# One more VectorE add, and two fewer TensorE sums, at the five stage changes of a two-layer encoder

## What is computed

```python
def _rmsnorm(x, g):
    xf = x.astype(jnp.float32)
    y = xf * lax.rsqrt(jnp.mean(xf * xf, axis=-1, keepdims=True) + EPS)
    return (y * g.astype(jnp.float32)).astype(x.dtype)
...
u = _modulate(_rmsnorm(x, norm_g[l, 0]), ada[:, 0], ada[:, 1])
x = x + 0.5 * ada[:, 2][:, None, :] * _swiglu(u, w_ff1_up[l], w_ff1_down[l])
```

## Time and profile before

| what | value |
| --- | --- |
| median of 3 runs | 2010.5 us (2010.05 to 2010.67) |
| the profiled execution's own time | 2011.53 us |
| its span in the profile | 2009.7 us |
| TensorE busy | 1997.3 us (99%) |
| VectorE busy | 986.4 us (49%) |
| ScalarE busy | 570.9 us (28%) |
| GpSimd busy | 679.6 us (34%) |
| granted TensorE clock | full level (2.4 GHz) until all of its work is done |

### The profile page before, as it was taken

The page is one execution under the profiler, slowest core; times in us unless marked ns, Lnnn a source line. Parts: engine busy times, 40 slices in busy tenths (PEclk is TensorE's granted clock), DMA queues, the critical chain, the costliest instruction groups (busy, mean ns, idle before and its releaser), DMA issues.

```text
span 2009.7 us, 24346 instructions
## 1 busy us (share of the span) xinstructions
PE 1997.3 (99%) x10051; PEld 1674.6 (83%) x10051; DVE 986.4 (49%) x1407; ACT 570.9 (28%) x837; POOL 679.6 (34%) x278
## 2 busy tenths in 40 slices
PE   8999999999999999999999999999999999999999
PEld 7888888987788888888898888889777898888888
DVE  4964265574465775312266624747643757211121
ACT  3221223234423322122242212224253233211221
POOL 1644346201000445444434644451200006443441
PEclk9999999999999999999999999999999999999999
DMA  9765366422234466333426645663222335323331
GB/s 298 206 213 171 89 198 207 101 74 84 63 99 132 126 187 210 84 105 100 131 84 196 204 134 147 174 202 77 78 74 69 121 105 157 121 82 100 86 119 60
DMA packets 351966, 264.75 MB, mean 132 GB/s; under 512 B 49966, under 2 KB 333794, under 8 KB 351856
## 3 DMA queue, kind: packets, MB, share of 16 engines
q1 hardware_dynamic: 350176, 262.70, 44.0%
q10 hardware_dynamic: 1392, 0.39, 0.1%
q0 software_dynamic: 288, 0.11, 0.0%
HBM read 261.07 MB, written 2.10 MB: 131 GB/s over the span
## 4 chain that ended last, share of the span: by engine, by line
PE 96%; DMA 1%; SPq 1%; DVE 1%; ACT 0%; issue 0%; DVEq 0%; ACTq 0%
PE bank L1535 28%; PE bank L1537 28%; PE bank L1536 28%; PE bank L1620 1%; PE bank L1624 1%; PE bank L1621 1%; PE bank L1562 1%; PE bank L1564 1%; PE bank L1563 1%; PE ps L1740 1%; DMA ada_block<-in_w_ada 1%; PE ps L1719 0%; PE ps L1728 0%; PE ps L1709 0%; SPq L559 0%
## 5 line engine op out<-in xcount | busy, mean ns | idle before, releaser
L660 POOL TENSOR_TENSOR w_lo<-stage,w_hi 128x1024 fp32r<-128x1024 f32 (+1 forms) x236 | 652.2, 2782 | 1158.6 <-ACT w_hi L720 1119.7
L1535 PE MATMUL bank<-u_hi,w_hi 128*128 128x512 f32 x1768 | 694.8, 393 | 1.4 <-DVE u_lo L1329 1.0
L1537 PE MATMUL bank<-u_hi,w_lo 128*128 128x512 f32 x1768 | 688.3, 389 | 0.0
L1536 PE MATMUL bank<-u_lo,w_hi 128*128 128x512 f32 x1768 | 688.0, 389 | 0.0
L720 ACT ACTIVATE w_hi<-stage 128x1024 fp32r<-128x1024 f32 (+2 forms) x335 | 348.4, 1073 | 548.0 <-DMA stage<-in_w_ff_up 292.9
L1535 PEld LDWEIGHTS bank<-u_hi,w_hi 128*128 128x128 f32 x1768 | 331.9, 188 | 73.9 <-issue 3.5
L1537 PEld LDWEIGHTS bank<-u_hi,w_lo 128*128 128x128 f32 x1768 | 331.8, 188 | 69.9
L1536 PEld LDWEIGHTS bank<-u_lo,w_hi 128*128 128x128 f32 x1768 | 332.0, 188 | 69.5 <-issue 1.9
L1535 PE MATMUL bank<-h_hi,w_hi 128*128 128x512 f32 x744 | 289.4, 389 | 0.0
L1536 PE MATMUL bank<-h_lo,w_hi 128*128 128x512 f32 x744 | 289.4, 389 | 0.0
L1537 PE MATMUL bank<-h_hi,w_lo 128*128 128x512 f32 x744 | 289.4, 389 | 0.0
(11 more groups left out here) (218 smaller groups left out, 1429.0 us busy)
## 6 DMA issues: line engine op xcount, KB each, us to landing
stage<-in_w_ff_up SPq DMA_DIRECT2D x172, 512.0 KB
ada_stage<-in_w_ada SPq DMA_DIRECT2D x128, 512.0 KB, 5.2
stage<-in_w_ff_down SPq DMA_DIRECT2D x32, 1408.0 KB
stage<-in_w_in SPq DMA_DIRECT2D x16, 1024.0 KB
ada_block<-in_w_ada SPq DMA_DIRECT2D x8, 1024.0 KB, 11.8
stage<-in_w_out SPq DMA_DIRECT2D x8, 1024.0 KB
stage<-in_w_in SPq DMA_DIRECT2D x40, 128.0 KB
stage<-in_w_in SPq DMA_DIRECT2D x10, 512.0 KB
```

Source lines behind the costliest of these rows:

```text
L660: nc.gpsimd.tensor_tensor(stage_tile(w_lo, kind, n), t, hi_tile(n, depth(kind, n)), ALU.subtract).then_inc(lo_ready, 1)
L1535: mm(bank[n % BANKS][:, :], hi[:, k, :], rhs_hi(k), start=(k == order[0]), stop=False)
L1536: mm(bank[n % BANKS][:, :], hi[:, k, :], rhs_lo(k), start=False, stop=False)
L1537: last = mm(bank[n % BANKS][:, :], lo[:, k, :], rhs_hi(k), start=False, stop=(k == order[-1]))
```

## The change

Three things are changed. VectorE gets a new add: at the head of `to_next` it adds the square of block 7's first half to `sq_sum`. `norm_sum` for the first half then reads `sq_sum` alone and leaves line 1595's two sums out; for the second half it stays as it was. And the place of that sum in pass 2 is step k_n - 3 where it was step 5: that is k = 8 after a feed-forward stage and still k = 5 after mixing. The rest renumbers the semaphore `squares_added`, which now counts eight adds per stage.

```diff
-SUM_K, SPREAD_K, SUM_B_K, SPREAD_B_K = 5, 4, 2, 5
+SPREAD_K, SUM_B_K, SPREAD_B_K = 4, 2, 5
...
             def to_next(l, i, done):
+                add_squares(event(l, i) + 1, KT - 1)
                 stats(*divmod(event(l, i) + 1, 3), 0)
                 close_second(l, i, 0, done)
-                add_squares(event(l, i) + 1, KT - 1)
+                add_squares(event(l, i) + 1, KT)
                 normalise(*divmod(event(l, i) + 1, 3), lambda: close_second(l, i, 1, done))
...
-                frames = slice(0, S) if step < KT - 2 else slice(0, FH) if step == KT - 2 else slice(FH, S)
-                done = {KT - 2: KT - 3, KT - 1: KT - 3}.get(step, step - 1)
-                dve.wait_ge(squared, HX * (e - 1) + (KT + 1 if step == KT - 1 else step + 1))
+                frames = slice(0, S) if step < KT - 2 else slice(FH, S) if step == KT else slice(0, FH)
+                done = {KT - 2: KT - 3, KT - 1: KT - 2, KT: KT - 3}.get(step, step - 1)
+                dve.wait_ge(squared, HX * (e - 1) + step + 1)
                 if done > 0:
-                    dve.wait_ge(squares_added, (KT - 1) * (e - 1) + done)
+                    dve.wait_ge(squares_added, KT * (e - 1) + done)
...
-                        if e < 3 * DEPTH and p == 2 and k == SUM_K:
+                        if e < 3 * DEPTH and p == 2 and k == k_n - 3:
                             norm_sum(e, 0)
...
-                pe.wait_ge(squares_added, (KT - 1) * (e - 1) + KT - 2 + h)
+                pe.wait_ge(squares_added, KT * (e - 1) + KT - 1 + h)
                 for j in (2 * h, 2 * h + 1):
-                    mm(ps5[:, j:j + 1], sq_sum[:, j * P:(j + 1) * P], ones[:, :], start=(j == 2 * h), stop=False,
-                       skip_group_check=True)
+                    last = mm(ps5[:, j:j + 1], sq_sum[:, j * P:(j + 1) * P], ones[:, :], start=(j == 2 * h), stop=(h == 0),
+                              skip_group_check=True)
+                if h == 0:
+                    last.then_inc(norm_summed, 1)
+                    return
                 pe.wait_ge(squared, HX * (e - 1) + KT + 2 * h)
```

More of the change, by code:

```diff
@@ L727, in square @@
                 act.wait_ge(x_updated, x_before(*divmod(e, 3)) - HX + step + 1)
-                added = {KT - 1: KT - 2, KT: KT - 3, KT + 1: KT - 1}.get(step, step - 1)
+                added = {KT - 1: KT - 2, KT: KT - 3, KT + 1: KT}.get(step, step - 1)
                 if added > 0:
-                    act.wait_ge(squares_added, (KT - 1) * (e - 1) + added)
+                    act.wait_ge(squares_added, KT * (e - 1) + added)
                 nc.scalar.activation((squares if m else sq_sum)[:, frames], x_t[:, m, frames], ACT.Square
```

## The result

The changed kernel takes **2015.23 us** (median of 17 runs, 2013.16 to 2017.87) against 2010.55 for the kernel before (17 runs, 2010.02 to 2014.47): 1.0022 times as long, with a 95% interval of 1.0016 to 1.0028. That is 4.7 us more. It lies inside the range (2012.0 to 2015.6) but 1.4 above the forecast of 2013.8. The 0.2% (4.0 us) that I had called "the same" lies within the interval, so on which side of it the change falls is not told. The time is where rival 2, the clock, had put it (2015.1).

What follows compares the result with a forecast made beforehand. TensorE, busy 1997.3 of 2009.7 us, was taken to bound the kernel; the five stage changes summed 1.35 + 0.62 - 0.64 + 1.23 + 0.72 = +3.3 us on 2010.5, giving 2013.8 us, range 2012.0 to 2015.6.

Steps and rivals of the forecast that it cites:

- rival 2: TensorE's clock falls to 1.2 GHz in the new 2.4 us stall from feed-forward to mixing: 2015.1 us, chance 0.22.
- The cause and the sign: At the five stage changes TensorE waits for VectorE's late add, making the kernel slower by 3.3 us.
- some 6: Sign to look for: TensorE waits for the new add at all five stage changes, some 6 us in all.
- Change 1: First stage change, feed-forward to mixing: add held up by GpSimd's low part, stall of 0.58 traded for 2.4, +1.35 us.
- Change 3: Third stage change, feed-forward to feed-forward: GpSimd is done, the old wait and removed sums go, -0.64 us.
- Change 4: Fourth stage change, like the first but without a wait before: add ends behind GpSimd's low part, +1.23 us.
- Changes 2 and 5: Stage changes after mixing: add stands behind VectorE's own low part and two vectors, +0.62 and +0.72 us.
- The port: Price of the add beside GpSimd's low part: it ends 0.28 us behind that; alone it costs 0.42.
- the forecast without the clock: Main case, five stage changes with no clock fall: +3.3 us, 2013.8 us, own range 2013.2 to 2014.4, chance 0.55.
- the chance for slower by over 0.2%: Chance that the whole kernel gets slower by more than 4.0 us: 0.28.
- It wins at each change: Rival: the add also hides at the stage changes after mixing, -2.4 us at best, 2008.1 us, chance 0.02.

Runs made afterwards that it cites:

- number 4: Changed kernel with ScalarE's square of block 7's first half put ahead of its rounding of the weight tile after a feed-forward stage: 2009.34 us.
- number 6: Changed kernel with the new add after mixing issued ahead of VectorE's last low part and the two vectors: 2012.81 us.
- number 3: Changed kernel with extra matmuls, whose result nobody reads, ahead of TensorE's wait in the two long stalls (16 and 10): 2013.79 us.
- Number 1: Kernel before, with the first half's two-operand norm sum moved to step k_n - 3 and no new add on VectorE: 2009.31 us.
- number 7: Changed kernel with the square ahead of the weight tile after feed-forward stages and the add ahead of VectorE's low part after mixing: 2007.16 us.
- number 2: Changed kernel with the first half's norm sum back at step 5 at all five stage changes: 2019.29 us.

## Why the prediction was right or wrong

**The cause and the sign** held. The add comes late for the two reasons named, and the experiments take them apart: GpSimd's low part after a feed-forward stage (number 4), VectorE's own low part after mixing (number 6). TensorE waited for the add at all five changes, 5.7 us against the "some 6" named as a sign, and the sums of the squares (line 1595, now 1599) have 20 records instead of 40.

**Change 1**: "+1.35 us". The stall was as worked out (the add ends 0.28 behind GpSimd, TensorE 0.05 later), and with the clock held up number 3 measures +1.41. The changed kernel has +2.93.

**Change 3**: "-0.64 us", measured -0.62. Number 1 gives the same -0.62 without the add: here the gain is the place's, and what the two sums save goes into the wait for the add.

**Change 4**: "+1.23 us", measured +0.98, and +0.87 in number 3. The weight tile that sets GpSimd's start landed a little earlier against TensorE's stream in these executions than in that of before.

**Changes 2 and 5**: "+0.62 us" and "+0.72 us", measured +1.01 and +0.63. At change 2 the tile's transfer is at times late. I took the add's start from one execution and did not follow it back to a DMA; number 3 has +0.77 there.

**The port.** "An add of line 1082 that comes while a low part of line 660 runs ends 0.28 behind it": measured to the hundredth at change 1. The rule weighed with it (the Trainium skill, "SBUF — State Buffer", Who interferes with whom: the one that starts first has the port pair for its whole length, and order decides) is borne out in both directions, though not by number 4 alone. There the add takes 0.42 instead of 2.36 us, but it is over before GpSimd starts, so it only shows the add undisturbed. The other order stands elsewhere in the trace of the changed kernel, where an instruction of VectorE with two inputs starts 0.06 us ahead of a low part:

```profile
244.66 0.69 DVE L1174 TENSOR_TENSOR h_lo<-prod,h_hi 128x512 fp32r<-128x512 f32 x1
244.72 2.90 POOL L660 TENSOR_TENSOR w_lo<-stage,w_hi 128x1024 fp32r<-128x1024 f32 x1 [11.24 <-ACT w_hi L720]
```

VectorE has its usual 0.69 us, and the low part takes 2.90 instead of 2.34 to 2.40.

**The step that failed** is the choice among the cases. I gave the forecast without the clock 0.55, and rival 2 0.22, although my own row had a fall after a pause of that length. Rival 2's mechanism was right: a fall in the stall of change 1 and none at change 4. Its size was a little low: I had put the time at the lower clock at 1.5 to 2.5 us and the loss at 0.8 to 1.3, and the trace has 3.4 and 1.5. That its 2015.1 us lies so near the 2015.23 measured is in part luck, since 0.4 us more at change 2 and 0.25 less at change 4 nearly cancel as well. What was mis-sized is its chance. Three of the 17 runs lie at 2013.2 to 2013.5, where the forecast without a fall would put them, and most of the others near 2015.2. I read these as executions without and with the fall, which is not shown, as only one of them was profiled. The mean granted clock recorded for each execution speaks for it without settling it: it is 0.999 or 0.998 in 16 of the 17 and 1.000 in one of the three short ones, and 1.000 in ten of the eleven of number 3; a fall at the start, as in the profiled one, counts in it too. With the fall as the usual case the chance for slower by over 0.2%, 0.28, was too low.

**"It wins at each change"** (rival 3, -2.4) does not hold for the change as made, but it does for its idea: number 7 gets -3.5 in the profile by moving two instructions in their queues. It is more than -2.4 for two reasons. Four records fewer are worth 0.44 where nothing is waited for, not the 0.34 that I gave changes 2 and 5 in that rival, and at change 3 the add of block 6 is no longer held up.

## What to carry to other kernels

Moving a small operation from the busiest engine to an idle one pays only if its result is there when the busy engine asks. So look not only at how busy the new engine is but at what stands ahead in its queue at that moment, and at whether GpSimd's low part runs beside it. It pays to ask whether an instruction can be moved ahead of what blocks it: here that won 5.9 us (5.7) with the square and 2.4 us (2.3) with the add. And a new stall of TensorE as long as this one (2.3 us) is to be priced with a fall of the clock in it, 1.5 or 3 us more, not as a side case.

## What was not expected of the hardware

- The clock fell behind a stall of 2.3 us, during the 0.6 us of tiny sums that followed, and stayed at 1.2 GHz for 3.4 us (389.5 to 392.9). It cost 1.5 us. In number 2 at change 4 it stayed low from about 1380.4 to 1387.3 us, and that change lost 5.34 us where I had put the stall alone at 2.3. At change 1 of number 6 the same stall of 2.3 us had the longer kind too (6.8 us, +4.29 instead of +1.35). So in these profiles a fall cost 1.5 us or about twice that, and the length of the stall did not tell which.
- Useless matmuls in a stall are worth time: 26 of them won 1.2 to 1.4 us.
- An add held up by GpSimd's low part needs less time behind it than it takes alone: it ends 0.28 us after it at changes 1 and 4, as in the earlier trace rows, though it takes 0.42 by itself.
